# Stick-breaking attention: TensorE takes the value products of a pair ahead of the next pair's tail products

## What is computed

```python
def stick_breaking_attention(h, w_qkv, w_o):      # 16 heads of 64
    ...
    z = jnp.einsum('bqhd,bkhd->bhqk', q[:, start:end], k[:, :end]).astype(jnp.float32) * scale
    strict = jnp.arange(end)[None, :] < jnp.arange(start, end)[:, None]
    log_one_minus = jnp.where(strict, jax.nn.log_sigmoid(-z), 0.0)
    tail = lax.cumsum(log_one_minus, axis=3, reverse=True) - log_one_minus
    weights = jnp.where(strict, jnp.exp(jax.nn.log_sigmoid(z) + tail), 0.0)
    outs.append(jnp.einsum('bhqk,bkhd->bqhd', weights.astype(v.dtype), v[:, :end]))
    ...
    return o @ w_o
```

## Time and profile before

| | us |
|---|---|
| median of 3 runs | 2088.29 |
| lowest and highest run | 2087.94, 2091.82 |
| the profiled execution, its own time | 2090.42 |
| its span in the profile | 2088.8 |
| mean granted TensorE clock in it | 0.946 |

### The profile page before, as it was taken

The page is one execution under the profiler, slowest core; times in us unless marked ns, Lnnn a source line. Parts: engine busy times, 40 slices in busy tenths (PEclk is TensorE's granted clock), DMA queues, the critical chain, the costliest instruction groups (busy, mean ns, idle before and its releaser), DMA issues.

```text
span 2088.8 us, 26100 instructions
## 1 busy us (share of the span) xinstructions
PE 1861.2 (89%) x10454; PEld 1642.7 (79%) x10454; DVE 1329.5 (64%) x1148; ACT 1006.8 (48%) x865; POOL 404.0 (19%) x433
## 2 busy tenths in 40 slices
PE   6989999067778999999998989999998899999997
PEld 6979998033347898888887789999887688888886
DVE  4425554068854688888885644443542688888886
ACT  4454333021114576666664433333445566666664
POOL 5328999834420000000000000000001000000000
PEclk9999999578789899999999989999999899999998
DMA  8614655312234699999996403544550499999993
GB/s 288 207 32 164 210 182 180 91 48 76 76 123 132 225 321 321 319 322 330 323 319 207 148 24 131 181 163 160 172 202 31 135 323 329 329 321 319 321 321 138
DMA packets 248275, 430.42 MB, mean 206 GB/s; under 512 B 6504, under 2 KB 210320, under 8 KB 248192
## 3 DMA queue, kind: packets, MB, share of 16 engines
q1 hardware_dynamic: 243520, 414.64, 57.7%
q0 software_dynamic: 4672, 14.60, 2.2%
HBM read 419.77 MB, written 9.44 MB: 205 GB/s over the span
## 4 chain that ended last, share of the span: by engine, by line
PE 72%; POOL 12%; DVE 10%; ACT 3%; issue 2%; DMA 1%; DVEq 0%; POOLq 0%; SPq 0%; ACTq 0%
PE PS L271 19%; PE PS L273 19%; PE PS L272 19%; PE PS L1016 4%; DVE wlo L310 3%; DVE uu L1106 2%; POOL tg L933 2%; PE PS L1253 1%; POOL tg L936 1%; POOL tm L934 1%; POOL tm L935 1%; POOL tm L931 1%; DVE vvv L1125 1%; PE PS L1298 1%; POOL tm L932 1%
## 5 line engine op out<-in xcount | busy, mean ns | idle before, releaser
L310 DVE TENSOR_TENSOR wlo<-raw,whi 128x3072 fp32r<-128x3072 f32 (+3 forms) x279 | 870.4, 3127 | 346.8 <-ACT whi L303 345.8
L303 ACT ACTIVATE whi<-raw 128x3072 fp32r<-128x3072 f32 (+3 forms) x279 | 708.4, 2540 | 421.7 <-PE PS L273 420.0
L271 PE MATMUL PS<-wlo,hT_hi 128*128 128x384 f32 (+3 forms) x1936 | 635.0, 328 | 15.5 <-DVE hT_lo L1505 3.4
L273 PE MATMUL PS<-whi,hT_hi 128*128 128x384 f32 (+3 forms) x1936 | 628.6, 325 | 0.0
L272 PE MATMUL PS<-whi,hT_lo 128*128 128x384 f32 (+3 forms) x1936 | 628.4, 325 | 0.0
L271 PEld LDWEIGHTS PS<-wlo,hT_hi 128*128 128x128 f32 x1936 | 368.3, 190 | 28.2 <-DVE wlo L310 6.9
L272 PEld LDWEIGHTS PS<-whi,hT_lo 128*128 128x128 f32 x1936 | 368.5, 190 | 3.7 <-issue 0.7
L273 PEld LDWEIGHTS PS<-whi,hT_hi 128*128 128x128 f32 x1936 | 368.1, 190 | 0.3
L423 POOL TENSOR_TENSOR stat<-stat,cst 128x1 f32<-128x1 f32 x18 | 14.9, 832 | 815.7 <-DVE stat L400 809.6
L271 PE MATMUL PS<-wlo,mhi 128*128 128x512 f32 x352 | 143.3, 407 | 16.4 <-DVE mlo L1518 16.4
L272 PE MATMUL PS<-whi,mlo 128*128 128x512 f32 x352 | 139.1, 395 | 0.0
(11 more groups left out here) (306 smaller groups left out, 2425.9 us busy)
## 6 DMA issues: line engine op xcount, KB each, us to landing
raw<-in_moe_w_gate_up SPq DMA_DIRECT2D x96, 1536.0 KB, 7.2
raw<-in_moe_w_down SPq DMA_DIRECT2D x48, 1536.0 KB, 7.1
raw<-in_ffn_w_gate_up SPq DMA_DIRECT2D x28, 1536.0 KB, 6.9
raw<-in_moe_w_gate_up SPq DMA_DIRECT2D x32, 1024.0 KB, 6.2
raw<-in_ffn_w_down SPq DMA_DIRECT2D x14, 1536.0 KB, 6.4
raw<-in_sb_w_qkv SPq DMA_DIRECT2D x12, 1536.0 KB, 7.5
raw<-in_moe_w_down SPq DMA_DIRECT2D x16, 1024.0 KB, 6.3
s_tables<-tg POOLq DMA_DIRECT2D x16, 512.0 KB, 3.8
```

Of the source, the lines that this page charges most:

```text
L271: pe.matmul(o, sh, mlw, start=start, stop=False, skip_group_check=True)
L273: return pe.matmul(o, sh, mh, start=False, stop=stop, skip_group_check=True)
L303: act.activation(whi[p0 % SPL][:, 0:n], raw[p0 % RAW][:, 0:n], ACT.Copy).then_inc(hi_done, 1)
L310: dve.tensor_tensor(wlo[p0 % SPL][:, 0:n], raw[p0 % RAW][:, 0:n], whi[p0 % SPL][:, 0:n].bitcast(F32), ALU.subtract).then_inc(lo_done, 1)
```

## The change

In the loop of TensorE's program, values(i-2) is called ahead of tails(i-1) instead of behind it. Nothing else differs: the two functions, their waits and signals, and the programs of the other engines are the same.

```diff
@@ -591,10 +591,10 @@
                     scores(i)
                 if i == 1:
                     keep_warm(pe, 7, 2)
+                if i >= 2:
+                    values(i - 2)
                 if 1 <= i <= PAIRS:
                     tails(i - 1)
-                if i >= 2:
-                    values(i - 2)
             pe.wait_ge(at_ol, PAIRS * (a + 1))
             proj_pe(pe, b0 + 9)
```

## The result

| | before | after |
|---|---|---|
| median | 2088.29 us (5 runs, 2087.56 to 2091.82) | 2100.23 us (5 runs, 2098.63 to 2102.58) |
| ratio, 95% interval | | 1.0056 (1.0041 to 1.007) |
| profiled execution: its time, its span | 2090.42, 2088.8 | 2099.47, 2097.9 |

What follows compares the result with a forecast made beforehand. No engine was full; a loop of handovers set the pace, 4.10 us a pair. Seven steps of 4.57 to 4.59 instead of 27.38 us add 4.7 for each attention, 9.4 in all: 2097.7 us, range 2093.0 to 2102.5.

Steps and rivals of the forecast that it cites:

- 0.88 + 0.82 + 0.81 + 2.06: New loop within one pair: pw to mask, to value products, to tail products, to pw; 4.57 us a pair.
- The one handover that the trace of before did not have: On TensorE, value products to tail products: taken as 0.81 us from value products to scores; alternatives 0.66 or 0.86.
- 0.66: Lowest value for value products to tail products, if weights load early; would give 4.2 us each attention, 2096.7 in all.
- two loops: Attention loop: one closing within a pair, 4.57 us, and the old one over two pairs, 4.59 a pair, against 4.10.
- The remark that the mask of pw stands 0.72 behind that of sp: GpSimd masks sp first, pw 0.72 us later; value products ahead of tail products must wait for the later mask.
- The sum: Whole kernel: 4.7 us for each of two attentions, 9.4 us more; 2097.7 us against the median.
- The places of the waits: TensorE: value products (L582) would wait for GpSimd's mask, about 0.9 us in each of eight; tail products (L565) hardly any.
- The rival that nothing changes: TensorE starts tail products past the waiting value products, so the time stays 2088.3 us; chance 0.03.
- A later end finds no more buffers filled than now: Weight queue behind the attention: raw buffers already full, so nothing gives the delay back; cover costed at nothing.
- The sign that was set too tight: Sign of being wrong: a later stage starts less than 4.7 us later than in the kernel before.
- The clock: Rival ahead of the projection: TensorE's clock falls, 1.5 us lost for each attention, up to 2100.7 us; chance 0.20.
- one gap of 1.8 us: TensorE idle between the last pair's tail products and value products: 1.8 us instead of 0.9, then 0.95 as before.

Runs made afterwards that it cites:

- after_again: The changed kernel, unaltered, run and traced once more; span 2097.5 us, first to last tail products 31.94 us in both attentions.
- before_again: The kernel before, unaltered, run and traced once more; span 2084.9 us, first to last tail products 27.37 us in both attentions.
- early_scores_warm: early_scores with one dummy matmul in each of the two gaps ending each attention; 2087.49 us against 2087.59 for the kernel before, ratio 0.9995.
- last_old: The changed kernel with the old order in iteration 8 alone (tail products of pair 7 ahead of value products of pair 6); span 2091.3 us.
- early_only: The kernel before with TensorE alone reordered to tails(i-1), scores(i+1), values(i-2); ScalarE and VectorE as before; span 2083.1 us.
- early_scores: The kernel before with TensorE taking tails(i-1), scores(i+1), values(i-2), and ScalarE and VectorE taking hT_hi and hT_lo one pair later; ratio 0.9995.
- before_mask_late: The kernel before with two dummy GpSimd masks ahead of the mask of pw, making it about 0.72 us later; span 2089.2 us.

## Why the prediction was right, and where it was not

**The loop.** Forecast 4.57 us a pair from 0.88 + 0.82 + 0.81 + 2.06; measured 4.56 to 4.57 from the same four steps, 31.95 us where 32.0 to 32.1 was forecast. Taking the difference from the measured 27.38 was needed: 7 times (4.57 - 4.10) would be 3.3 us, since the seven steps of before do not average 4.10; the first of them took 2.82. The one handover that the trace of before did not have, value products to tail products, is 0.81 (114.72 to 115.52, 119.28 to 120.09: 0.80 and 0.81), the value taken. The Trainium skill's rule on weight loads pulled ahead ("TensorE: Matmul & The Clock Gate", "Architectural detail") would have given 0.66 as I used it; the trace does not bear that out. The 0.66 was no fit measure in any case: it is the length of the L582 rows alone, and the L583 rows of the same value products start 0.48 behind them and end only 0.88 behind their start (119.76 and 0.40 long).

**Which loop decides.** I held two loops for nearly equal and based the steps on 7 times 4.57 to 4.59. The experiments separate them: the loop within one pair sets the pace (4.56 with GpSimd's order swapped, 5.28 with the mask 0.72 later). The remark that the mask of pw stands 0.72 behind that of sp was true of the old trace but is not what costs in the new one, where it starts 0.88 behind its pw. The sum was not touched by this.

**The places of the waits** moved as forecast: 0.87 us ahead of the value products, none ahead of the tail products but the first. The rival that nothing changes falls with it: TensorE did not take the tail products past the waiting value products. The Trainium skill, same page, section "The mechanism", says that matmuls run strictly first in, first out; the trace agrees, with eight waits ahead of L582 and no L565 started in one of them.

**Behind the loop.** "A later end finds no more buffers filled than now": held. The expert stage has the same TensorE busy time within 0.2 us in 50. The next work of GpSimd behind the first attention, in the norm (L423), shows how the delay arrives there; before, after and after_again:

```profile
159.53 0.55 POOL L423 TENSOR_TENSOR stat<-stat,cst 128x1 f32<-128x1 f32 x1 [26.48 <-DVE stat L400]
```

```profile
165.51 0.55 POOL L423 TENSOR_TENSOR stat<-stat,cst 128x1 f32<-128x1 f32 x1 [28.03 <-DVE stat L400]
```

```profile
164.06 0.55 POOL L423 TENSOR_TENSOR stat<-stat,cst 128x1 f32<-128x1 f32 x1 [26.48 <-DVE stat L400]
```

That is 30.19 us behind the last tail products before (159.53 - 129.34), 30.18 in after_again (164.06 - 133.88) and 31.73 in after (165.51 - 133.78): without the fall the loop's delay arrives whole and alone, with it 1.5 us more. Behind the second attention the step is the same (31.12, 31.11 and 32.68 us), but the end of the span is not so clean: from the last tail products it is 498.4 us in both executions of the kernel before, 499.1 in after_again and 499.8 in after. So nothing of the loop's delay was absorbed, but only half of the 1.5 us of the clock shows between the two executions of the changed kernel, and 0.7 us has another cause. The traces show a likely one: TensorE's clock is low again from some 45 us behind the last tail products, and by the granted clock of the windows there it is back at 2.4 GHz 59.0 us behind them in before, 61.2 in after_again and 60.8 in after. TensorE is busy at the end of that stretch, so two more us at half speed would make about one. No run isolates that.

**The sign that was set too tight.** I named as a sign of being wrong that a later stage starts less than 4.7 us later. Without the fall it does: L423 is 4.53 us later in after_again than in before (164.06 - 159.53). The 4.7 was near the top of my own 4.6 to 4.75, and it left no room for the measured 4.57; this sign could not tell the theory from its rounding.

**The clock** is the step that was given too little. I forecast one gap of 1.8 us and gave a fall in at least one attention 0.20. There are two such gaps in a row, since iteration 8 has no scores to fill the one ahead of the value products of pair 6, which I overlooked; and the profiled execution had the fall in both attentions. The price was right (1.5 forecast, 1.54 measured). Of the two executions of the changed kernel one had it, and of the five with the new order at the end and no dummies four had it at least once: it was no rare case.

**The sum.** Measured 11.9 us (8.6 to 14.6) against 9.4. The two loops make 9.1 of it (twice 4.57), seen in both executions. The clock adds up to 1.54 for each fall, none to two of them in an execution. With 6 falls in 10 attentions that would be 1.8 us on average (an estimate from 2 x 0.6 x 1.54); the remaining microsecond is not settled and lies within the interval. The profiled executions show how much else moves: between the last tail products of the first attention and the first of the second it takes 1433.7 us in before and 1429.9 in before_again, the same kernel, and 1432.4 and 1432.6 in the two executions of the changed one. That scatter of nearly 4 us is why the clock's share had to be read in the trace, and it can hide most of the 3 us of early_scores_warm; that it does is not shown.

## What to carry to other kernels

An operation that waits for another engine should not stand ahead of one that is on the path and needs nothing from it: here 0.8 us of matmuls moved ahead of the tail products made a loop of four handovers that must close once in every pair, instead of a longer one that closes once in two. To price a new order, write down the loops that it closes, add their steps from rows of the trace, and divide each by the number of turns that it spans; and look separately at the first and last iterations, where some of the work that fills the gaps is missing.

## What the hardware showed that I had not expected

The clock that TensorE gets in the stretch behind a sparse end is not fixed by the kernel. The same program with the same idle times (3.71 us busy of 7) had 0.52 in one execution and 1.00 in the next. Gaps of 0.93 and 0.95 us at the end of the loop were followed by full clock in all 8 attentions of before, before_again, last_old and early_only, and by the low one in both of early_scores; before_mask_late, with 1.6 and 0.95 us, had full clock in both. The Trainium skill, "TensorE: Matmul & The Clock Gate", section "What's actually happening", says that the clock follows how busy the engine has been, and that the slow start of one kernel differs from run to run. The traces agree: the fall too differs between executions of one kernel, and a single profile is not enough to charge it to an edit.
